# Where the first two expert blocks get their rows, and when their up product runs

## The reference, cut to what matters

```python
def moe_ffn(x2d, w_router, b_router, w_up, b_up, w_down, b_down):
    logits = (x2d @ w_router) + b_router
    top_v, top_e = lax.top_k(logits, TOP_K)          # 4 of 32
    gates = jax.nn.softmax(top_v, axis=-1)
    ...                                              # rows sorted by expert, cut in blocks
    def expert_block(args):
        xb, e = args
        hh = xb @ w_up[e] + b_up[e]                  # 1024 -> 2048
        return clamped_swiglu(hh) @ w_down[e] + b_down[e]   # 1024 -> 1024
```

## Time and profile before

| | us |
|---|---|
| median of 3 runs (lowest, highest) | 1372.64 (1372.63, 1376.26) |
| the profiled execution, device time | 1375.49 |
| its span, first to last instruction | 1373.7 |
| TensorE busy | 1302.8 (95%) |
| VectorE busy | 924.7 (67%) |
| ScalarE, GpSimd busy | 278.9, 122.6 |
| DMA: bytes moved, mean rate | 468.38 MB, 341 GB/s |
| mean granted clock of TensorE | 0.985 |

### The profile page before, as it was taken

How to read it: one execution, slowest core, us unless ns; L and a number is a source line. 1 busy time by engine, 2 the same in 40 slices (tenths; PEclk the granted TensorE clock), 3 DMA queues, 4 the chain that set the end, 5 groups by cost and what they waited for, 6 DMA issues and landing times.

```text
span 1373.7 us, 21478 instructions
## 1 busy us (share of the span) xinstructions
PE 1302.8 (95%) x6329; PEld 528.1 (38%) x6329; DVE 924.7 (67%) x1885; ACT 278.9 (20%) x529; POOL 122.6 (9%) x228
## 2 busy tenths in 40 slices
PE   8999999998898999998999999899999997999997
PEld 6866565553332333332233332233333331333332
DVE  3225246646776777785778778577877875787788
ACT  4231133421211112121212112121211211121122
POOL 2000000000110110110011011001101100110100
PEclk9999989998999999999999999999999999999998
DMA  9405162046799999999999999999999999999995
GB/s 363 111 4 186 31 217 105 31 184 238 277 407 422 421 412 423 420 422 420 409 420 410 416 417 421 416 420 409 421 415 421 412 421 422 419 406 421 410 416 221
DMA packets 90878, 468.38 MB, mean 341 GB/s; under 512 B 11854, under 2 KB 28992, under 8 KB 40546
## 3 DMA queue, kind: packets, MB, share of 16 engines
q1 hardware_dynamic: 74542, 441.04, 79.2%
q0 software_dynamic: 7360, 16.79, 3.2%
q10 hardware_dynamic: 8948, 10.19, 2.1%
HBM read 623.20 MB, written 28.25 MB: 474 GB/s over the span
## 4 chain that ended last, share of the span: by engine, by line
PE 71%; DMA 22%; DVE 3%; SPq 2%; issue 1%; ACT 1%; DVEq 0%; ACTq 0%
PE ps L1957 33%; DMA raw<-in_w_down_dram 21%; PE ps L1996 17%; PE ps L1641 5%; PE ps L1618 5%; PE ps L1857 4%; SPq L577 2%; DMA w_a_cols<-in_w_in_dram 1%; PE ps L1812 1%; PE ps L1811 1%; PE ps L1885 0%; PE ps L1720 0%; PE ps L1803 0%; DVE v_gate L1210 0%; DVE h L1216 0%
## 5 line engine op out<-in xcount | busy, mean ns | idle before, releaser
L1957 PE MATMUL ps<-raw,xT 128*64 128x512 f32 x2880 | 633.4, 594 | 24.7 <-DMA raw<-in_w_up_dram 21.0
L1445 DVE STREAM_TRANSPOSE xT<-x_hold 32x64 f32<-32x64 f32 (+1 forms) x704 | 282.8, 402 | 165.6 <-PE ps L1957 145.0
L1957 PEld LDWEIGHTS ps<-raw,xT 128*64 128x64 f32 x2880 | 204.7, 137 | 446.5 <-issue 398.8
L1996 PE MATMUL ps<-raw,aT 128*64 128x512 f32 x1440 | 324.7, 595 | 18.4 <-DMA raw<-in_w_down_dram 18.1
L1445 DVE STREAM_TRANSPOSE aT<-act_g 32x256 f32<-32x256 f32 x360 | 228.4, 634 | 69.3 <-PE ps L1996 59.2
L1996 PEld LDWEIGHTS ps<-raw,aT 128*64 128x64 f32 x1440 | 99.7, 137 | 236.4 <-issue 177.3
L914 ACT ACTIVATE act_s<-act_g 128x512 f32<-128x512 f32 x46 | 29.0, 630 | 659.2 <-DVE act_g L1429 659.2
L533 POOL DMA_INDIRECT slot_outputs<-y_rows,out_idx x44 | 45.2, 1028 | 651.4 <-ACT y_rows L919 651.4
L1262 DVE STREAM_TRANSPOSE bias_up<-up_cols 128x1024 f32<-128x1024 f32 x47 | 58.5, 1245 | 1.6
L525 POOL DMA_INDIRECT x_rows<-expert_inputs,row_idx x48 | 50.4, 1049 | 79.1 <-DVE row_idx L1332 42.3
L1857 PE MATMUL ps<-w_out_sb,mixT 128*128 128x512 f32 x128 | 56.8, 598 | 0.6 <-DVE mixT L1199 0.6
(11 more groups left out here) (373 smaller groups left out, 869.7 us busy)
## 6 DMA issues: line engine op xcount, KB each, us to landing
raw<-in_w_up_dram SPq DMA_DIRECT2D x368, 1024.0 KB
raw<-in_w_down_dram SPq DMA_DIRECT2D x184, 1024.0 KB, 10.5
slot_outputs<-zeros ACTq DMA_DIRECT2D x1, 8320.0 KB, 28.0
raw<-slot_outputs SPq DMA_DIRECT2D x8, 1024.0 KB, 16.0
w_c_cols<-in_w_in_dram SPq DMA_DIRECT2D x1, 4096.0 KB, 31.0
w_out_sb<-in_w_out_dram SPq DMA_DIRECT2D x1, 4096.0 KB, 13.6
w_a_cols<-in_w_in_dram SPq DMA_DIRECT2D x1, 2624.0 KB, 13.1
x_sb<-in_x_prompt_dram SPq DMA_DIRECT2D x4, 512.0 KB, 5.3
```

Source lines behind the costliest of these rows:

```text
L1445: dve.transpose(dst_at(rows_out, group), src_at(rows_in, parity)).then_inc(done, 1)
L1957: ins = mm(ps[SUB * i:SUB * i + SUB, banks[bank], :], rows_in[:, j, :], raw[:, SLOT[j], c:c + HF], start=False, stop=(j == UPU - 1), skip_ ...
L1996: ins = mm(ps[SUB * i:SUB * i + SUB, 2, :], aT[:, j, r, :], raw[:, units[j], D * r + HF * i:D * r + HF * i + HF], start=False, stop=(j == ...
```

## The change

- **Block 0** takes expert 0's rows among the first `EARLY_TILES` = 4 tiles (0 to 3), up to 64. Its positions (`early_positions`, `early_list`), list and gather are made inside the last tile's output product. If fewer than 64 are found, the places left are empty: `early_pad` of them. The positions of the last tile's rows and the count of expert 0 are raised by as much.
- **Block 1** is always expert 0's places 65 to 128; the count is raised to at least 65 for that. Its list needs no table, and its weights aren't loaded again.
- **Block 0's up units** are issued one by one (`first_up(j)`): unit 0 with the turned rows before `turn_h2` of the last tile, the others between the router's steps, 4 and 5 to 7 around `find(1)`. The identity products go.
- **Block 2's** list is found during block 1 (`find_third`, `find(2)`, `gather(2)`), and TensorE turns its rows. Blocks 1 and 2 are taken out of TensorE's loop, with `down(0)` ahead of block 2. `destinations`, `placements`, `place` and `lists` come after block 1's up product.
- Banks are assigned anew, the table gets room for one block more, and the last 128 rows of `xn_dram` are cleared.

In the diff `find`, `mark_written`, `turn_rows` and `indices` are moved up unchanged but for the parts shown; the lines left out are these, bank numbers, and steps that only count.

```diff
 SUB = 64
-MAXBLK = NE + TOK * TOPK // SUB
+MAXBLK = NE + TOK * TOPK // SUB + 1
+EARLY_TILES = PT
...
-        FIRST_BANKS, TURN_BANKS = (7, 4), (3, 6)
...
+        POS_BANK, ORDER_BANK, TABLE_AT = 4, 6, 2 * NE
+
...
-                if isinstance(b, int) and b in (1, 2):
+                if isinstance(b, int) and b in (1, 2, 3):
                     pool.wait_ge(x0_psum, 2 * b)
                 elif not (isinstance(b, int) and b == 0):
...
             gather(0)
+            pool.wait_ge(h2_stored, 16 * NTILE)
+            gather(1)
+            gather(2)
             pool.wait_ge(mixer_left, 4)
-            gather(1)
             pool.wait_ge(lists_ready, 1)
-            gather(2, own)
...
                     sp.dma_start(raw[:, SLOT[UPU + j], :], src, cond=cond).then_inc(landed[UPU + j], 16)
 
+            for j in range(UPU):
...
             sp.wait_ge(lg_psum, NTILE)
-            sp.wait_ge(gathered, 16)
             for j in range(DNU):
+                if j == 2:
+                    sp.wait_ge(gathered, 2 * 16)
                 load_down(0, j, None)
             sp.wait_ge(table_made, 1)
             nb = block_count(sp)
-            e_up, new_up = expert(sp, 1), is_new(sp, 1)
-            for j in range(UPU):
-                sp.wait_ge(up_used, j + 1)
-                load_up(e_up, j, new_up)
             sp.dma_start(g_final_bc[:], g_final.rearrange("(a n) -> a n", a=1).to_broadcast([P, D])).then_inc(ld_gfinal, 16)
...
+                act.dma_start(xn_dram[SEQ - P:SEQ, :].rearrange("p (h x) -> p h x", h=4),
+                              bc(zeros[:], 1, [P, 4, 2 * P])).then_inc(slots_cleared, 16)
...
 
+            def seed_up(b, banks):
+                act.wait_ge(up_staged, b + 1)
...
+            def take_turned(b, dst):
+                for a in range(2):
...
                     move_pT(1)
+                if t == PT:
+                    act.wait_ge(banks_written, 2)
+                    seed_up(0, FIRST_BANKS)
+                    take_turned(0, xT_first)
...
             act.sem_inc(y_ready, 1)
-            act.wait_ge(banks_written, 2)
-            seed_up(0, FIRST_BANKS)
-            for b, dst in ((0, xT_first), (1, xT)):
-                if b:
...
-            act.wait_ge(banks_written, 4)
+            act.wait_ge(banks_written, 3)
+            seed_up(1, (0, 1))
+            take_turned(1, xT)
+            sigmoid(0)
+            act.wait_ge(up_read, 1)
             seed_down(0)
-            sigmoid(0)
-            hold(2)
+            sigmoid(1)
+            act.wait_ge(up_used, 2 * UPU)
+            take_turned(2, xT)
+            act.wait_ge(up_read, 2)
+            seed_up(2, (0, 1))
+            y_out(0)
+            seed_down(1)
+            act.sem_inc(x_held, 2)
+            hold(3)
             act.wait_ge(table_made, 1)
             nb = block_count(act)
-            with act.Fori(1, nb) as b:
+            with act.Fori(2, nb) as b:
                 sigmoid(b)
                 act.wait_ge(up_read, b + 1)
...
+            def indices(b):
+
+                dve.wait_ge(list_psum, b + 1)
+                if b:
+                    dve.wait_ge(gathered, 16 * b)
+                do(dve.tensor_reduce(found[:], ps[:, 5, 0:4], AX, ALU.add))
+                dve.tensor_scalar(row_idx[:], found[:], far_half[:], None, ALU.add).then_inc(idx_ready, 1)
+
+            def early_list():
+
+                dve.wait_ge(pos_psum, 1)
+                step(dve.scalar_tensor_tensor(early_pos[:].unsqueeze(2), ps[:, 0, 0:EARLY_TILES].unsqueeze(2), 1.0,
+                                              m_keep[:, 0:EARLY_TILES, 0:1], ALU.add, ALU.mult))
+                step(dve.tensor_scalar(early_pad[:], ps[:, 0, EARLY_TILES:EARLY_TILES + 1], float(SUB), -1.0, ALU.min, ALU.mult))
+                settle()
+                compare(early_pos[:].unsqueeze(2), EARLY_TILES)
+                do(dve.tensor_scalar(early_pad[:], early_pad[:], float(SUB), None, ALU.add))
+                indices(0)
+
...
+                dve.wait_ge(cols_made, 3)
+                pick_columns(own, 0, 0)
+                stage_up().then_inc(up_staged, 2)
+                stage_down().then_inc(down_staged, 2)
 
             take_gla(0)
...
                     mask_gla(t + 2)
-                if t == 2:
-                    dve.wait_ge(outputs, 4 * 16)
...
 
...
                                         m_keep[:], ALU.add, ALU.mult))
-            compare(pos_table[:, :, 0:1])
...
-            count = ps[:, 0, NTILE * NE:(NTILE + 1) * NE]
-            for m in range(EXTRA):
-                step(dve.tensor_scalar(over[:, m, :], count, float(SUB * (m + 1)), None, ALU.is_gt))
+            do(dve.scalar_tensor_tensor(pos_table[:, PT, 0:1], m_keep[:, PT, 0:1], early_pad[:], pos_table[:, PT, 0:1],
...
+
+            count = ps[:, POS_BANK, NTILE * NE:(NTILE + 1) * NE]
+            step(dve.tensor_copy(counts[:, 1:NE], count[:, 1:NE]))
+            step(dve.tensor_scalar(counts[:, 0:1], count[:, 0:1], early_pad[:], float(SUB + 1), ALU.add, ALU.max))
             step(dve.memset(one_hot[:, 0, :], 1.0))
             settle()
-            indices(0)
+            for m in range(EXTRA):
+                step(dve.tensor_scalar(over[:, m, :], counts[:], float(SUB * (m + 1)), None, ALU.is_gt))
+            settle()
+            indices(1)
             many = over[:, 0, :]
...
             dve.wait_ge(mixer_left, 4)
...
 
-            find_second()
+            clamp(0, FIRST_BANKS)
+            indices(2)
+            swiglu(own, 0)
+            turn_a(0, aT)
+            dve.wait_ge(aT_ready, 8)
+            clamp(1)
+            dve.wait_ge(up_staged, 2)
+            dve.wait_ge(down_staged, 2)
+            pick_columns(own, expert(dve, 2), 0)
+            dve.wait_ge(up_seeded, 2)
+            stage_up().then_inc(up_staged, 1)
+            swiglu(own, 1)
             destinations()
-            indices(1)
             for k in range(TOPK):
                 placements(k)
-            dve.sem_inc(up_read, 1)
             lists()
-            dve.wait_ge(up_staged, 1)
-            dve.wait_ge(down_staged, 1)
-            pick_columns(own, expert(dve, 1), 0)
-            dve.wait_ge(up_seeded, 1)
...
             last = scattered_blocks(dve)
-            with dve.Fori(1, last) as b:
+            with dve.Fori(2, last) as b:
                 STEPS = 3
-                o = Own(dve, dve_own, b * STEPS + (before_loop - STEPS))
...
                     pe.wait_ge(mixT_ready, 2 * t + k // 4 + 1)
+                    if t == PT and k == 2:
+                        early_positions()
+                    if t == PT and k == 5:
+                        find(0, EARLY_TILES)
+                    if t == PT and k == 6:
+                        mark_written(FIRST_BANKS)
                     for n in range(2):
...
 
-            def keep_busy(n):
-                for i in range(n):
-                    mm(ps[:, 1, :], ident[:], t_x2[1][:, 0:4 * P], start=True, stop=True)
+            def early_positions():
+                pe.wait_ge(routed, EARLY_TILES)
+                for t in range(EARLY_TILES + 1):
+                    dst = ps[:, 0, t:t + 1]
+                    for i in range(t):
+                        ins = mm(dst, ones_b[:], m_keep[:, i, 0:1], start=(i == 0), stop=(i == EARLY_TILES - 1))
...
+                ins.then_inc(up_used, 1)
+
+            def first_up(j):
+                if j == 0:
+                    pe.wait_ge(up_seeded, 1)
+                if j in (0, 4):
+                    pe.wait_ge(xT_ready, 8 + 2 * j)
+                pe.wait_ge(landed[j], 32)
+                up_products(j, xT_first, FIRST_BANKS)
 
...
                     attend(t + 1)
                 else:
-                    keep_busy(4)
+                    turn_rows(0)
+                    first_up(0)
                 turn_h2(t)
                 if t + 2 < NTILE:
                     score(t + 2)
+                if t == PT:
+                    first_up(1)
                 router(t)
+            first_up(2)
             sum_parts(PT)
-            keep_busy(1)
-
-
...
-            find(0)
-            mark_written(FIRST_BANKS)
...
+            first_up(4)
+            find(1)
+            for j in range(5, UPU):
+                first_up(j)
+            mark_written((0, 1))
...
+                        pe.wait_ge(xT_ready, 24 + 2 * j)
+                    up_products(j, xT, (0, 1))
+                    if j == 4:
+                        find(2)
+
+            def third_up():
+                pe.wait_ge(up_seeded, 3)
+                for j in range(UPU):
+                    if j in (0, 4):
+                        pe.wait_ge(xT_ready, 40 + 2 * j)
+                    pe.wait_ge(landed[j], 48)
+                    up_products(j, xT, (0, 1))
+                    if j == 4:
+                        place()
 
...
 
             pe.sem_inc(dn_used, 2 * DNU)
             table()
-            first_up()
+            second_up()
+            turn_rows(2)
+            down(0, aT, SLOT[UPU:])
```

(43 more changed lines are left out.)

160 lines of the change are left out of this document (58 added, 102 removed).

## The result

The changed kernel takes 1386.09 us (median of 4 runs, 1382.51 to 1388.24), the kernel before beside it on the same chip 1372.85 (4 runs, 1372.63 to 1376.26). The ratio is 1.0093, 95% interval [1.0076, 1.0111]: it is **slower by 0.9%**. The forecast was 1362.0, with a chance of 0.85 for faster. The profiled execution took 1384.1 us, its span is 1382.3, against 1373.7 before.

The account below looks back on a forecast made before the run. The stream of expert weights through full DMA engines was taken as the bound: U3 12.5 us earlier, less 1.9 lost at block 4's slot, gives 10.6, so 1372.64 becomes 1362.0; range 1356 to 1368, over 0.8.

Parts of the forecast that it names:

- U2: SP's load of block 2's up unit 0, first new weights: to go out at 340.6 us, 14.5 earlier.
- U3: SP's next load of new weights, after down(0): to go out at 365.4 us, 12.5 earlier.
- Blocks, last product, router, block 1: Mixer's end to block 1: 46 blocks stay, product ends at 310.3, positions 4.5 late, block 1 starts at 335.1, 16.6 earlier.
- The index for block 1's gather: After the router's chain: the index comes at 327.2 us, against 321.64 before.
- table: VectorE's table after the order product: ready at 335.8 us, 5.8 late.
- The third gather: Block 2's rows, ahead of down(0): lands 6.5 us after issue, at 351.8; down(0) ends at 361.7, clock charge 1.9.
- down(1): Block 1's down product: waits 2.5 us for VectorE's turning of activations and ends at 387.3.
- Given back later: Block 4's late weight slot, block 3 starting at 392.6: DMA queue empty, 1.9 us lost, bounds 0 and 5.
- Rival 1: At the seam more is kept: faster gather, block 3 by 390, U2's 14.5 us count; 1358; chance 0.10.
- Rival 2: VectorE's serial chain between 366 and 393 delays block 3 to 396, 5 us lost; 1365; chance 0.14.
- Rival 3: The third gather lands behind U2's weights at 363.5, U3 goes at 377; no change, 1372; chance 0.07.
- Rival 4: TensorE's clock stays at half through blocks 1 to 3, block 3 ending some 45 us later; 1400; chance 0.05.

Follow-up runs that it names:

- e1: Changed kernel with the clear of the last 128 rows of xn_dram issued by ScalarE in tile 2, not right behind the slots' clear: 1365.10 us, ratio 0.9948.
- e2: Changed kernel with the two clears in the other order, the 512 KB one before the 8320 KB one: 1364.85 us, ratio 0.9935.
- e8: Changed kernel with half of the slots' clear (4160 KB, from 64 partitions) ahead of the second clear, the other half in tile 2: 1378.3 us, one run.
- the five kernels: The changed kernel and four variants that leave its seam between mixer and experts unchanged: mean 1107.6 us from third store to end, against 1118.9.

## Why the prediction was wrong

It was wrong by 24 us, and on the wrong side, and nearly all of it is **one term that it left out**: an issue on ScalarE's queue, taken as costing nothing, that held the engine for 20.45 us. By the ratios, the changed kernel (1.0093) is 1.45 to 1.58% above e1 and e2 (0.9948, 0.9935), 20 to 22 us. The other 2 to 3 us are the seam: e1 and e2 are 8.1 and 8.3 us faster than the kernel before, 10.6 were forecast.

"The change, part by part" goes through blocks, product, router, block 1, U2 and U3, and has no line for the clear of `xn_dram`'s last rows, which stands in the list of the change and in the diff: one more DMA issued by ScalarE. Nor did the reading reach there: the argument began at 299 us, the stall is at 188.

Both halves of the warning stood in the trace of before. The first clear, 8320 KB, landed 28 us after an issue of 0.60, on the queue of an engine whose next copy TensorE needed within 3 us. And whether an issue behind a large transfer returns at once or is held could be read from SP's queue, where one of 128 KB took 14.60 (rows under e8). So the bounds of that term were 0.6 and 28 us, and 20.45 falls between. With that range the forecast could not have been 0.85 for faster.

The steps that it did take, each as measured in the changed kernel less 18.24, then as forecast:

- *Blocks, last product, router, block 1*: 46 blocks; the product ends at 309.2, forecast 310.3; block 1 starts at 334.1, forecast 335.1. Right, about 1 early, which is already there at the product's end: what was put into it cost 0.9, charged 2.0.
- *The index for block 1's gather*: 344.14 + 0.21 less 18.24 = 326.1, forecast 327.2; the *table* 352.82 + 0.19 less 18.24 = 334.8, forecast 335.8. Right.
- *U2*: 339.2, forecast 340.6. Right: the added reads of registers cost SP 4.4 after the table (357.45 - 353.01), forecast 4.8.
- *The third gather* landed 7.4 after its issue, forecast 6.5, TensorE waited 3.38, forecast 2.7, and down(0) took 8.39, forecast 8.77. The list was found 1.2 early (342.8, forecast 344.0), and so the errors cancel: down(0) ends at 361.5, forecast 361.7. That this one is right to 0.2 is luck. The clock of this gap (0.50 from 372 to 374) cost 1.5 in the chain of waits (8.32 - 6.87), charged 1.9.
- *down(1)*: it ends at 390.6, forecast 387.3. It waited 3.01, forecast 2.5, and then took 9.99 where 7.04 is full speed, at a granted clock of 0.50 from 398 to 402: the forecast charged the clock for the gap ahead of down(0) and left it out here. It cost nothing, as block 3 waited for VectorE anyway, and block 3's own 13.95 had 15.65 charged.
- *U3*: 365.2, forecast 365.4: 12.7 earlier against the third store, forecast 12.5.
- *Given back later*: 1.5 at block 4's slot, forecast 1.9, with block 3 at 392.4, forecast 392.6. 9.7 came of 12.7 in this pair of executions, so 3.0 went, of which 1.5 has no place; but the mean gain of the five kernels is 11.3, and 1.5 is within what single executions differ by.
- *Rival 1* (more is kept): no. *Rival 2* (VectorE gives more back): no, block 3 is where it was forecast. *Rival 3* (the gather behind the weights): no, 7.4. The rule of the Trainium skill cited there ("DMA: Bandwidth & Descriptors", section "Queues, rings and completion order"), that each DMA engine takes turns between queues, agrees with that landing. *Rival 4* (the clock): its place was wrong. The longest new idle time was in the mixer, where half clock cost 1.7 us behind it, and behind the gaps ahead of down(0) and down(1) it cost 1.5 and 3.0. After each the clock came back with TensorE at work (0.96 from 210 to 212, 1.00 from 374 to 378 and from 406 on), and the whole is no 45 us. None of the four is the cause.

So the mechanism at the seam was right, to within 1.4 us at every step but down(1), and the sum lacked a cost of some 20 us that is not of the seam.

The Trainium skill speaks of issuing twice. "DMA: Bandwidth & Descriptors", section "Issuing engines are not separate DMA queues", has the time to initiate a DMA as "usually small relative to the DMA itself"; here it was 0.54 to 0.65 for the clears that stood behind nothing large, but 20.45 for the same 512 KB behind 8320 KB, and 20.42 for 128 KB: the measurement decides. The same page's section "Rules for kernel authors" advises to issue a DMA early, compute, and wait on its semaphore late. Both clears follow that, and it is the early issue itself that waited.

## What to carry to other kernels

Count each added DMA as an instruction of the engine that issues it, and look at what is already in that engine's queue: behind a transfer of thousands of packets the issue held the engine here, whatever its own size, so put the small one first or on a queue with room. Look in the trace for issues that take several us: they show where it happens already. Read the whole diff against the whole span; a line far from the change's subject can outweigh it. And where a stream of weights bounds the kernel, count what its pauses cost: starting it earlier pays only as far as its next slots come free in time.

## What of the hardware was unexpected

- An issue on ScalarE's queue held the engine for 20.45, 20.44, 20.42 and 14.76 us and returned with 1604, 1610, 1614 and 1564 packets of 1 KB left of the clear ahead of it. On SP's queue, issues of the kernel before were held up to 14.60 us, and returned with some 1240 to 1450 packets left.
- The hold is of one queue: SP's issues took 0.30 and 1.14 us while ScalarE's queue had over 5200 packets left.
- The clear to DRAM from 64 partitions moved at 189 GB/s, from 128 at 348, both in 1 KB packets and with the DMA engines' share near 1: a share of 1 doesn't mean full rate.
- A gather issued into a full stream landed after 7.4 us, a little beyond the 6.5 to 7.3 of the earlier trace rows.
